# Expert pairs of the second token tile, spread otherwise over the first tile's attention and MLP

## What is computed

```python
u_e = u[experts]                     # 128 rows of 1024 for each token
v_e = v[experts]                     # 128 rows of 1024 for each token
a = jax.nn.gelu(jnp.einsum('td,thkd->thk', xb, u_e))
return jnp.einsum('thk,thkd->td', (g * a), v_e)
```

```python
x = first_block(...)                 # ends in rmsnorm(x + g2 * peer(...), final_g)
u = rms_norm(h, norm_pre_mix)        # start of the second block
ff = jnp.square(jax.nn.relu(v @ w_up)) @ w_down
h = h + rms_norm(ff, norm_post_mlp)
```

## Time and profile before

| | us |
|---|---|
| median of three runs | 1498.22 (1493.79 to 1500.22) |
| profiled execution | 1497.28 |
| its span in the trace | 1495.5 |
| TensorE matmul busy | 1230.8 |
| VectorE busy | 883.5 |
| ScalarE busy | 494.4 |
| GpSimd busy | 286.8 |
| DMA, mean over the span | 341 GB/s |

### The profile page before, as it was taken

The page is one execution under the profiler, slowest core; times in us unless marked ns, Lnnn a source line. Parts: engine busy times, 40 slices in busy tenths (PEclk is TensorE's granted clock), DMA queues, the critical chain, the costliest instruction groups (busy, mean ns, idle before and its releaser), DMA issues.

```text
span 1495.5 us, 19519 instructions
## 1 busy us (share of the span) xinstructions
PE 1230.8 (82%) x7108; PEld 873.1 (58%) x7108; DVE 883.5 (59%) x1781; ACT 494.4 (33%) x1226; POOL 286.8 (19%) x296
## 2 busy tenths in 40 slices
PE   6999989999888859745766555777899998899997
PEld 4888565555443328635643442555688975647775
DVE  1769557877799866589969896645412535501003
ACT  3104424323323343334544651311222343612114
POOL 0120023443343432223312232221000000000000
PEclk6999999999999889977978687899999999999999
DMA  9875279999999999999999999999988674278884
GB/s 380 332 245 224 113 284 384 422 426 427 426 427 426 426 405 405 424 426 396 426 425 391 372 350 394 392 426 423 385 284 300 219 279 147 109 255 293 292 304 177
DMA packets 71706, 510.11 MB, mean 341 GB/s; under 512 B 8112, under 2 KB 8256, under 8 KB 10688
## 3 DMA queue, kind: packets, MB, share of 16 engines
q0 software_dynamic: 40400, 290.02, 47.4%
q1 hardware_dynamic: 30640, 216.78, 38.1%
q10 hardware_dynamic: 576, 2.10, 0.4%
HBM read 507.82 MB, written 1.05 MB: 340 GB/s over the span
## 4 chain that ended last, share of the span: by engine, by line
PE 45%; DMA 20%; DVE 17%; issue 10%; ACT 5%; POOL 1%; SPq 0%; another core or an unknown queue 0%; DVEq 0%; ACTq 0%; POOLq 0%
PE bank L1147 9%; DMA ring<-in_weights 9%; DMA arena<-in_experts,arena 9%; PE bank L1157 6%; PE bank L1213 5%; PE bank L1121 5%; PE bank L1177 4%; DVE arena L2263 3%; PE bank L805 3%; PE bank L817 3%; DMA junk<-in_experts,arena 3%; PE bank L1074 2%; DVE arena L2270 2%; DVE arena L2282 1%; PE bank L991 1%
## 5 line engine op out<-in xcount | busy, mean ns | idle before, releaser
L1147 PE MATMUL bank<-act_t,ring 128*128 128x128 f32 x2048 | 255.2, 287 | 26.0 <-DMA ring<-in_weights 16.4
L1147 PEld LDWEIGHTS bank<-act_t,ring 128*128 128x128 f32 x2048 | 249.4, 202 | 45.5 <-issue 37.1
L1121 PE MATMUL bank<-arena,diag 128*128 128x512 f32 x512 | 240.3, 621 | 33.4 <-ACT diag L1655 32.5
L1121 PEld LDWEIGHTS bank<-arena,diag 128*128 128x128 f32 x512 | 97.6, 198 | 160.5 <-issue 109.6
L2263 DVE SCALAR_TENSOR_TENSOR arena<-arena,bank 128x1024 f32<-128x1024 f32 x128 | 153.2, 1220 | 49.9 <-DMA arena<-in_experts,arena 48.6
L2270 DVE SCALAR_TENSOR_TENSOR arena<-arena,bank 128x1024 f32<-128x1024 f32 x109 | 132.6, 1217 | 81.9 <-DMA arena<-in_experts,arena 81.6
L711 POOL DMA_INDIRECT arena<-in_experts,arena x128 | 127.5, 996 | 270.6 <-PE bank L1121 162.4
L737 POOL DMA_INDIRECT arena<-in_experts,arena x109 | 113.3, 1039 | 330.8 <-DVE arena L2282 297.4
L1157 PE MATMUL bank<-ring,act_t 128*128 128x256 f32 x704 | 162.0, 390 | 13.2 <-DMA ring<-in_weights 8.6
L1157 PEld LDWEIGHTS bank<-ring,act_t 128*128 128x128 f32 x704 | 136.0, 195 | 37.1 <-issue 7.2
L2282 DVE SCALAR_TENSOR_TENSOR arena<-arena 128x1024 f32<-128x1024 f32 x108 | 138.3, 1281 | 4.8 <-ACT arena L1675 4.5
(11 more groups left out here) (311 smaller groups left out, 1660.0 us busy)
## 6 DMA issues: line engine op xcount, KB each, us to landing
ring<-in_weights SPq DMA_DIRECT2D x200, 1024.0 KB
arena<-in_ada_weights POOLq DMA_DIRECT2D x16, 1024.0 KB, 7.8
arena<-in_experts,arena POOLq DMA_INDIRECT x237, 14.0
arena<-in_rpb POOLq DMA_DIRECT2D x4, 512.0 KB, 15.4
arena<-in_weights SPq DMA_DIRECT2D x2, 1024.0 KB, 7.9
row<-in_rows_in ACTq DMA_DIRECT2D x3, 512.0 KB, 3.8
res<-in_x SPq DMA_DIRECT2D x1, 1024.0 KB, 9.6
arena<-in_ctx_in SPq DMA_DIRECT2D x1, 1024.0 KB, 8.5
```

The costliest lines, as they stand in the source:

```text
L1121: last = mm(bank(j), diag[:, k % 4, :], bufs[k % N_BUF][:, D + half * 512:D + half * 512 + 512], start=(k == 0), stop=(k == SLOTS - 1))
L1147: last = mm(b[:, at + m * P:at + m * P + P], w[:, c, m * P:m * P + P], act_t[:, c, t * P:t * P + P], start=(c == 0), stop=(c == C - 1))
```

## The change

Pairs 2 to 63 get other beats. Before, they stand evenly over beats 3 to 110. Now a table gives each stretch of beats a number of pairs: 33 over beats 2 to 58, 5 over 59 to 74 (where 9 stood), 8 over 75 to 87 (8 before), and 16 over 88 to 116 (13 before, up to 110). So the last pair moves from MLP step 11 to step 13. ScalarE's two first norms of tile 1, which stood in MLP steps 13 and 14, come behind the last step, and the load of `row1` moves from step 12 to step 15, into another slot buffer, the one with slots 2, 9, ... 121.

```diff
-        ROW1_BUF = 4
+        ROW1_BUF = 2
...
-        LAST_BEAT = 112
         PAIRS = SLOTS // GROUP
         EARLY = 2
+        STAGES = ((2, 59, 33), (59, 75, 5), (75, 88, 8), (88, 117, 16))
+        PAIR_BEATS = [a + i * (b - a) // n for a, b, n in STAGES for i in range(n)]
+        assert len(PAIR_BEATS) == PAIRS - EARLY
 
         def pairs_at(beat):
-            return [g for g in range(EARLY, PAIRS) if g * LAST_BEAT // PAIRS == beat]
+            return [EARLY + n for n, at in enumerate(PAIR_BEATS) if at == beat]
...
-                    if (t, k) == (0, MLP_N - 4):
+                    if (t, k) == (0, MLP_N - 1):
                         act.wait_ge(freed1[ROW1_BUF], len(range(ROW1_BUF, SLOTS, N_BUF1)))
                         act.dma_start(row1, rows_in[0:1, :].broadcast_to([P, D])).then_inc(row1_loaded, 16)
-                    if (t, k) == (0, MLP_N - 3):
-                        first_norm(3, 1)
-                    if (t, k) == (0, MLP_N - 2):
-                        first_norm(4, 1)
+                if t == 0:
+                    first_norm(3, 1)
+                    first_norm(4, 1)
                 if t:
                     load_root()
                 take_sums("mlp", t, own.side)
```

## The result

| | us |
|---|---|
| kernel before, median of 11 runs beside the changed one | 1497.15 (1493.79 to 1501.14) |
| changed kernel, median of 11 runs | 1514.24 (1505.95 to 1519.52) |
| ratio, with its 95% interval | 1.0120 (1.0104 to 1.0137) |
| forecast | 1497.0 (1485 to 1508) |
| span of the profiled execution, before and after | 1495.5, 1512.6 |

What follows compares the result with a forecast made beforehand. No single engine bounds the kernel; where the pairs move, DMA at 424 GB/s does. Terms +4.0 + 2.0 - 2.8 - 6.0 + 1.4 = -1.4 us against 1497.28 gave 1495.9, with the median at 1497 us, range 1485 to 1508.

Steps and rivals of the forecast that it cites:

- The extra pair ahead of the attention costs bytes, not idle, and is in the ledger: Ahead of the attention: one more pair adds DMA bytes there but no DMA idle, so no term of its own.
- the ledger: From 545 us to tile 1's first unit: unchanged bytes at 424 GB/s plus DMA's idle time, 32.2 us of 553.
- The opening, +2.0: Pair 2 ahead of the turned tile starts TensorE's first unit 4.67 us later; DMA idle grows 2.0 us, between 0 and 4.7.
- The attention, 53.2 us: Attention shrinks from 68.6 to 53.2 us with four pairs fewer; DMA idle there rises from 9.9 to 13.9, +4.0.
- The output projection, -2.8: With pair 50's place behind the norm empty, TensorE's 5.43 us wait shrinks by about 3; idle -2.8 us, at worst 0.
- MLP, 134 us to the last dot's end: MLP start to last dot's end goes from 109.6 to 134 us: six more slots, less one place; rate unchanged.
- The tail, -6.0: Last dot's end to tile 1's first unit: 17.7 us, 29 units loaded at its start, idle 1.5 instead of 7.5 us.
- the norms come into the open: Rival, 22%: slots land late, the ring is full at the last dot's end, the tail idles 7.5 us; 1504.4 us.
- The clock, +1.4: Behind the tail, TensorE's matmuls start at half clock after idling; +1.4 us outside the ledger, between 0 and 2.75.
- Slower: the attention stays long: Rival, 14%: the four pairs' time turns into waits, attention 63 us, term +13.8 instead of +4.0; 1507 us.
- Faster: Rival, 26%: attention comes near its bytes at 43 to 45 us, term -4.2 instead of +4.0; 1489 us, down to 1483.
- No change that can be measured: Case, 38%: the attention's gain is paid back at DMA's rate; own range 1491 to 1504 us.

Runs made afterwards that it cites:

- run 5: Changed kernel with pair 32 alone moved from beat 53 to 54, pair 33 staying at 55: 1509.53 us, 1.0069 of the kernel before.
- run 9: Kernel before with only pair 31 moved from beat 54 to 53: 1507.93 us, 1.0073 of the kernel before.
- run 10: Kernel before with eight pairs in the attention, fourteen in the MLP, none at beat 87, norms at their old steps: 1497.04 us, 0.9997.
- run 1: Changed kernel with pair 32 moved from beat 53 to 54 and pair 33 from 55 to 56: 1505.00 us, 1.0066 of the kernel before.
- run 2: Changed kernel with pairs 2 to 33 at their old beats and six pairs in the attention instead of five: 1502.49 us, 1.0050 of the kernel before.
- run 6: Kernel before with only pair 50 moved from beat 87, behind the norm, to beat 86: 1497.64 us, 0.9982 of the kernel before.
- run 8: Against the kernel before: pairs 2 to 33 at old beats, seven in the attention, fifteen in the MLP, norms late: 1501.32 us, 1.0005.
- run 3: Kernel before with only the two first norms moved behind the last MLP step: 1495.86 us, 1.0015 of the kernel before.
- run 7: Against the kernel before: pairs 2 to 33 at old beats, eight in the attention, fourteen in the MLP, norms late: 1503.06 us, 1.0035.
- run 4: Changed kernel with its 16 MLP pairs ending at beat 109, norms at steps 13 and 14, row load at step 12: 1519.30 us, 1.0167.

## Why the prediction was wrong

- **"The extra pair ahead of the attention costs bytes, not idle, and is in the ledger": this step failed.** It counted the pair and not its place. Beat 53 lies on ScalarE between two copies that had followed each other at once, and TensorE waits for the second. Idle +13.2 us in the changed kernel, where I had 0; with its pair moved off beat 53 the ratio falls from 1.0120 to 1.0069, 7.6 us (run 5), and in the kernel before one pair moved onto it costs 0.73%, 10.9 us (run 9). That is shown from both sides. Of run 9's 10.8 us in the rope stretch, 7.2 are the later start of the last rope matmuls (17.2 us behind the first ones instead of 10.0), 4.1 the slower small matmuls up to the `w_out` units, and 2.1 those units; 2.6 come back in a shorter wait ahead of the first scores. Only the first of these is the place's for certain: the other three stand in run 10 too, which has no pair at beat 53 and 38.1 us, and against run 10 the stretch of run 9 is 7.7 longer. In the same way the rope stretch idles 5.6 to 7.7 us in runs 1, 2, 5, 6, 8 and 10, against 2.9 before and 16.1 in the changed kernel, so some 8 to 10 of the 13.2 are beat 53's.
- **The opening, +2.0:** measured -0.4. The first rope matmul came 7.8 us later than before, relative to slot 0's dot, and nearly all of it is bytes, the ledger's view. A small error.
- **The attention, 53.2 us:** 53.4 by the forecast's own cut, from the first max to the last item normalised (833.4 to 886.8); the 60.0 of the ledger ends at the `w_out` unit. Right in length. VectorE's waits for the scores, 7.4 + 5.4 = 12.8 in the forecast, are one group of the view of lines:

```profile
L2556 DVE TENSOR_TENSOR bank<-bank,arena 128x512 f32<-128x512 f32 x8 | 5.6, 695 | 12.0 <-PE bank L1402 12.0
```

- Idle there grew by 6.5 instead of 4.0 (by the forecast's cut, at 303 GB/s, to 15.2 us from 9.9). DMA moved 301 GB/s, "below 330" as said.
- **The output projection, -2.8:** -2.5. The wait fell from 5.43 to 2.07 us. Right, and run 6 shows the wait alone.
- **MLP, 134 us to the last dot's end: failed.** It took 146.0. The forecast took six slots more and one place less. Two rows that wait for a slot at about the same distance from the MLP's start, of before

```profile
974.86 1.22 DVE L2270 SCALAR_TENSOR_TENSOR arena<-arena,bank 128x1024 f32<-128x1024 f32 x1 [0.98 <-DMA arena<-in_experts,arena]
```

and of after

```profile
971.65 1.22 DVE L2271 SCALAR_TENSOR_TENSOR arena<-arena,bank 128x1024 f32<-128x1024 f32 x1 [2.51 <-DMA arena<-in_experts,arena]
```

- stand 20.7 and 20.3 us behind the MLP's start. Counted from the end they are slots 109 and 102. So seven more had to come through the shared part, not five: two at 4.98 are 10 of the 12 us. The rate per slot was right. The "one place less" was wrong: in run 6, where pair 50 alone moves, the last dot ends 113.8 us behind the MLP's start and not sooner than before (110.8; run 3, with pair 50 in its old place, has 112.2). The other slot is in the ledger. Up to the MLP's start DMA had idled 41.0 of 404.5 us, against 24.2 of 404.9 before, so it had moved 17.2 us of transfers less, seven and not six. What held the seventh back wasn't tried; run 2 has 145.3 us with the rope stretch mended, so beat 53 doesn't explain it.
- **The tail, -6.0: failed with it.** Its length is right in its own steps (residual 6.7 us behind the last dot's end, as said; 16.0 to the first unit against 17.7), but the ring was nearly full. This is the rival "the norms come into the open" with its own signs: 33 units loaded, a tail of 16.1, 7.5 us idle; measured 33.5, 16.0, 8.8. It gave 1504.4, a ratio of 1.0048 to the 1497.15 of before, near what runs 1, 2 and 5, without the pair at beat 53, measured (1.0066, 1.0050, 1.0069). Its condition, "if slots land later than I count", came true, and I had it at 22%.
- **The clock, +1.4:** the rest of the program took 1.7 more, and tile 1's first 256 matmuls are 1.5 of it (30.32 us, the first 3.1 at a granted 0.50, against 28.82 at 1.00). Right. The Trainium skill, TensorE: Matmul & The Clock Gate, section What's actually happening, states that the half clock is the default and activity releases it; the trace agrees here, where TensorE had stood 3.24 and 1.27 us, and at the rope matmuls: granted 0.50 behind 2 us of work in 13.
- **"Slower: the attention stays long"** didn't come: 53.4 us by the forecast's cut. **"Faster"** didn't either, and its ground, the attention near its bytes at 43 to 45 us, fell: with five pairs it has 17.4 us of idle, and from seven pairs to five it wins 4.3 us of 9.3.
- **No change that can be measured** is what runs 8 and 10 give, so the argument that the attention's win is paid back at DMA's rate fits one or two pairs. Run 7, one pair with the norms late, is 0.35% slower, and why it should be slower than run 8 isn't shown. The argument breaks at the third pair, where the tail has too little time left to load weights in.

By the ledger the four largest misses, 13.2 + 7.4 + 2.5 - 2.4, make 20.7; with 2.5 less ahead of slot 0's dot that is 18.2 of the 18.5 between -1.4 and the span's +17.1.

## What to carry to other kernels

When filler work gets one more place, look at each new place on every engine's own queue: between which two instructions it comes, what its first wait is, and who waits for the instruction behind it. Here the one place that split two adjacent copies cost 8 to 11 us, about twice the 4.67 of work that it holds. And a stage with slack at its end can take in deferred work only until that slack is used: count what is loaded when it ends, with the error of the count, before booking the gain.

## What the runs showed of the hardware

- The same part of the program comes out at two lengths, by the clock. Run 10 differs from the kernel before only behind the attention's start, and yet its rope stretch has 38.1 us instead of 35.0 (the window opens 1.0 us ahead of it):

```profile
779.60:818.70 39.10, 31.33 (x114) 18.80 (x114) 31.43 (x49) 13.03 (x28) 7.94 (x8) 0.73 0.87 343
```

- The difference arises behind the wait of 6.72 us, which is in every run. From the last rope matmuls to the `w_out` units TensorE has the same matmuls in the kernel before and in run 10, 2 large ones and 44 small ones, and no wait over 0.36 us. Before, the clock is back at nearly full; in run 10 it stays at 0.50, the lower level (1.2 of 2.4 GHz), though TensorE is busy for 9.74 of 10.10 us:

```profile
791.60:797.70 6.10, 5.74 (x48) 4.72 (x46) 5.71 (x9) 2.33 (x8) 0.05 (x1) 0.91 0.94 394
```

```profile
790.20:800.30 10.10, 9.74 (x48) 8.28 (x46) 9.66 (x15) 3.91 (x11) 1.23 (x3) 0.50 0.57 214
```

- So a stall can cost more than itself: the 44 small ones take 1.7 to 1.8 times as long (3.62 against 1.97 us for the last 16), and the 32 large ones behind 16.07 against 13.98, in runs 2, 6, 8 and 10 (16.22 in run 8) as in runs 4, 9 and the changed kernel (16.05 to 16.27). In the kernel before and runs 1, 3, 5 and 7 they don't. All three kernels with a pair at beat 53 have the slow form, four of nine without one: whether the second wait of 7 us makes it certain isn't shown, and what decides it otherwise isn't either.
- Over the whole rope stretch the granted clock is 0.73 in run 10, against 0.89 in the kernel before. Runs 2, 6 and 8 have 38.0 to 38.5 us, runs 1, 3, 5 and 7 have 35. One profiled execution is so uncertain by 3 us in this stage, and up to tile 1's first unit by less, as the ring makes up for some of it. The readings above that rest on single executions are to be taken with that; the ratios come from many. Run 9's 45.8 and the changed kernel's 46.5 lie far outside both.
- Two queues with transfers waiting shared DMA in halves, in the kernel before and in the changed one: slots of 1 MB came 4.93 to 4.98 us apart at a total of 424 GB/s.
